# Strassen's seven products on two of eight k pairs of a gate/up projection in a fused decoder layer

## The chip, the cores and the metric

One core of one Trainium2 chip runs the whole layer as one program. The metric is the device time of an execution in microseconds, median of three. TensorE multiplies (PE in the profile), ScalarE (ACT) and VectorE (DVE) prepare its operands, SyncE (SP) issues the loads of the weights from HBM, and GpSimd (POOL) has little to do.

## The reference

A decoder layer over 256 tokens with a model width of 2048. What the change touches is the SwiGLU part with `D_FF = 5632`:

```
hn = rms_norm(h, ffn_norm[i])
h = h + (jax.nn.silu(hn @ w_gate[i]) * (hn @ w_up[i])) @ w_down[i]
```

Before it stand the combined projection, the two head groups and `w_o`, behind it a gated embedding (`w_ple_gate`, `w_ple_proj`). All inputs and weights are float32.

## The kernel before, in words

Each float32 operand is split into a rounded part (`hi`, type fp32r) and the remainder (`lo`), and each product is made as three matmuls: hi·hi, hi·lo, lo·hi (`k_tile`, lines 559 to 561). The stationary operand of a matmul is a 128x128 piece of the transposed activations `xT_hi` or `xT_lo` (one k tile of 128 rows, one half of the tokens), the moving one a 128x512 piece of weights.

The weights come in **units**: two k tiles by 512 columns, 512 KB, one DMA each. A unit goes through a ring of four buffers: SP loads `raw`, ACT rounds it into `w_hi` (line 915), DVE subtracts to `w_lo` (line 1226), PE multiplies. SP may load unit u when DVE is done with unit u-4 (`lo_ready`), ACT may round unit u when PE is done with unit u-4 (`unit_used`), PE waits for `lo_ready` of its unit. ACT and DVE work three units ahead of PE (`LEAD`). A unit is 12 matmuls.

A **gate/up block** makes 512 columns of gate and of up: eight units of `w_gate` into the two PSUM banks `pair[0]` (one for each half of the tokens), then eight units of `w_up` into `pair[1]`. There are eleven blocks: six (`FF_A`), then their down projection, five (`FF_B`), and theirs. The first block of either stage is written out ("peeled"), the five and four others are the body of a hardware loop. Behind the gate's last unit ACT makes the sigmoid and DVE the SiLU into `gate_s` (lines 1171 and 1525), which frees `pair[0]`. Behind the block DVE multiplies by up into `act_s` (line 1531), which frees `pair[1]`. In the next block PE transposes `act_s` into two spare banks behind its fourth unit (`turn_act`, line 829), and ACT and DVE split the result (`turned`, lines 1154 and 1509). All engines execute their instructions in the written order, and semaphores join them; nothing is reordered by a scheduler.

Of the kernel before, what the change touches and what calls it, by code (L numbers as in the profile page):

```python
# [24 lines left out]
ALU = mybir.AluOpType  # L25
# [70 lines left out]
def plan():  # L96
# [75 lines left out]
LAST_PIECES = ((0, 0, CB), (1, 0, CB // 2), (1, CB // 2, CB))  # L172


def build(nc, A):
    FIRST, AT, BANK_OF = plan()

    with ExitStack() as ctx:
# [63 lines left out]
        pp = sb("pp", [P, NT, D], at=res + 16 * KIB)  # L242
        sq = [sb(f"sq{t}", [P, CB]) for t in range(NT)]
# [4 lines left out]
        p_in = sb("p_in", [P, NT, PLE])  # L248
        pT_hi = sb("pT_hi", [P, PLE // P, TOK], F32R)
# [70 lines left out]
        ff_full, ff_free = [sem("ff_full0"), sem("ff_full1")], [sem("ff_free0"), sem("ff_free1")]  # L320
        pg_mul, out_ready, pg_full = sem("pg_mul"), sem("out_ready"), sem("pg_full")
# [64 lines left out]
        def _(sp):  # L386
            def load(u, j, w, k, col):

                if not isinstance(u, int) or u >= RING:
                    sp.wait_ge(lo_ready, u - (RING - 1))  # L390
                sp.dma_start(raw[j % RING][:], w[:, k:k + KU, bass.ds(col, CB)]).then_inc(raw_landed[j % RING], 16)
# [156 lines left out]
        def _(pe):  # L548
# [282 lines left out]

            def gate_up(i, u0, b0, n0, peeled):

                for j in range(2 * UPB):
                    use(i * (2 * UPB) + (u0 + j))
                    bl = j // UPB
                    if j % UPB == 0:

                        pe.wait_ge(pair_free[bl], i * 2 + b0)
                    for kk in range(KU):  # L840
                        k = KU * (j % UPB) + kk
                        if peeled and n0 == 0 and k in (0, 12):
                            for g in (range(6) if k == 0 else (6, 7)):
                                wait_read(pe, ("hA", g))
                        last = k_tile(j, kk, xT_hi[:, k, :], xT_lo[:, k, :], pair[bl], k == 0, k == KT - 1)
                        if kk == KU - 1:
                            last.then_inc(unit_used, 1)
                        if peeled:
                            for s in AT[u0 + j][kk]:
                                burst(s)  # L850
                    if j == 3 and not peeled:
                        pe.wait_ge(pair_free[1], i * 2 + b0)
                        turn_act()

            for n, n0, ug, ud, bgt, bd in ((FF_A, 0, U_GUA, U_DA, B_GUA, B_DA), (FF_B, FF_A, U_GUB, U_DB, B_GUB, B_DB)):
                gate_up(0, ug, bgt, n0, True)
                with pe.Fori(1, n) as i:
                    gate_up(i, ug, bgt, n0, False)
                def turn_last():
                    pe.wait_ge(pair_free[1], bd)  # L860
                    turn_act()
# [42 lines left out]
        def _(act):  # L904
# [13 lines left out]
            def post(step, b, half=None):  # L918
# [237 lines left out]

            def gate_up(i, u0, b0, n0, peeled):
                for j in range(2 * UPB):
                    split(i * (2 * UPB) + (u0 + j + LEAD), j + LEAD)
# [6 lines left out]
                    if j == UPB - 1:  # L1166
                        act.wait_ge(h_rstd, 2)
                        act.wait_ge(unit_used, i * (2 * UPB) + (u0 + UPB))
                        act.wait_ge(pair_free[1], i * 2 + b0)
                        for t in range(NT):  # L1170
                            f(gate_s[t][:], pair[0][t][:], ACT.Sigmoid, scale=h_rs[0][:, t:t + 1]).then_inc(gate_sig, 1)
# [48 lines left out]
        def _(dve):  # L1220
# [15 lines left out]
            def post(step, b, half=None):  # L1236
# [7 lines left out]
                if step in ("x", "hA", "hB"):  # L1244
                    col = {"x": G_ATTN, "hA": G_FFN, "hB": G_PLE}[step]
                    dve.wait_ge(x_hi, hi_base[step] + 2 * b + (1 if half == 0 else 2))
                    for kk in (0, 1) if half is None else (half,):
# [263 lines left out]

            def gate_up(i, u0, b0, n0, peeled):
                for j in range(2 * UPB):
                    split(i * (2 * UPB) + (u0 + j + LEAD), j + LEAD)
# [6 lines left out]
                    if j == UPB - 1:  # L1521
                        dve.wait_ge(h_rstd, 2)
                        for t in range(NT):
                            dve.wait_ge(gate_sig, i * 2 + (2 * n0 + t + 1))
                            v.scalar_tensor_tensor(out=gate_s[t][:], in0=pair[0][t][:], scalar=h_rs[0][:, t:t + 1],
                                                   in1=gate_s[t][:], op0=ALU.mult, op1=ALU.mult).then_inc(pair_free[0], 1)
                    if j == 2 * UPB - 1:
                        dve.wait_ge(unit_used, i * (2 * UPB) + (u0 + 2 * UPB))
                        dve.wait_ge(pair_free[0], i * 2 + (b0 + 2))
                        for t in range(NT):  # L1530
                            v.scalar_tensor_tensor(out=act_s[t][:], in0=pair[1][t][:], scalar=h_rs[0][:, t:t + 1],
# [66 lines left out]
```

## Time and profile before

| | |
|---|---|
| median of 3 runs | 1337.19 us (1337.16 to 1338.31) |
| profiled execution | 1338.08 us |
| its span | 1336.1 us |
| busy, share of the span | PE 100%, DVE 59%, ACT 47% |
| HBM read | 235.36 MB, 178 GB/s |

The profiled execution is 0.9 us over the median; its span leaves 2.0 us of it outside. "Busy" of PE overlaps, since a matmul's record is longer than the distance to the next one, so the pace of PE is read from start to start.

### The profile page before, as it was taken

The numbers are of one execution on the slowest core, as the hardware profiler recorded it, in microseconds if no ns is written. First come the engines' busy times: TensorE is split into PE (matmuls) and PEld (weight loads), VectorE is DVE, ScalarE is ACT, GpSimd is POOL, SyncE is SP. The second block draws the span as 40 slices with busy tenths as digits, with TensorE's granted clock in tenths as the row PEclk, the third lists the DMA queues.
The fourth block names the chain that finished last, engine by engine and source line by source line (L and its number), as shares of the span: only waits on it lengthen the run. The fifth ranks groups of instructions, "written<-read, shape, count | busy, mean of one in ns | idle before, by whom it ended". The sixth has DMA issues, their size and how long they took to land.

```text
span 1336.1 us, 18200 instructions
## 1 busy us (share of the span) xinstructions
PE 1330.2 (100%) x6774; PEld 1100.3 (82%) x6774; DVE 789.3 (59%) x987; ACT 626.8 (47%) x788; POOL 53.6 (4%) x71
## 2 busy tenths in 40 slices
PE   9999999999999999999999999999999999999998
PEld 8788888887888888888888888888888888888887
DVE  6578885788585555555555554444555555555554
ACT  6576444543555545444444443334444444444543
POOL 4002000220000000000000000000000000000000
PEclk9999999999999999999999999999999999999999
DMA  8555544554444555665666555566656665555564
GB/s 267 173 178 169 149 142 136 153 154 138 131 130 150 187 190 181 197 190 188 188 190 189 187 188 194 193 198 190 189 189 189 188 187 189 188 189 187 191 191 141
DMA packets 126201, 238.35 MB, mean 178 GB/s; under 512 B 9711, under 2 KB 10786, under 8 KB 126138
## 3 DMA queue, kind: packets, MB, share of 16 engines
q1 hardware_dynamic: 126106, 237.48, 56.8%
q8 instruction: 43, 0.70, 0.2%
q14 instruction: 20, 0.16, 0.0%
q10 hardware_dynamic: 32, 0.01, 0.0%
HBM read 235.36 MB, written 2.10 MB: 178 GB/s over the span
## 4 chain that ended last, share of the span: by engine, by line
PE 99%; DMA 0%; DVE 0%; ACT 0%; issue 0%
PE pair L559 30%; PE pair L561 30%; PE pair L560 30%; PE bg L679 2%; PE bg L744 2%; PE bg L615 1%; PE bg L829 1%; PE bg L725 0%; PE bg L592 0%; PE pair L898 0%; PE pair L897 0%; PE pair L899 0%; PE bg L643 0%; PE bg L650 0%; PE bg L659 0%; DMA row_a<-in_attn_norm_dram 0%
## 5 line engine op out<-in xcount | busy, mean ns | idle before, releaser
L1226 DVE TENSOR_TENSOR w_lo<-raw,w_hi 128x1024 fp32r<-128x1024 f32 x442 | 540.1, 1225 | 420.7 <-ACT w_hi L915 417.8
L915 ACT ACTIVATE w_hi<-raw 128x1024 fp32r<-128x1024 f32 x442 | 467.1, 1059 | 487.1 <-PE pair L561 483.5
L559 PE MATMUL pair<-w_hi,xT_hi 128*128 128x512 f32 x1264 | 503.1, 398 | 0.0
L561 PE MATMUL pair<-w_hi,xT_lo 128*128 128x512 f32 x1264 | 493.3, 390 | 0.0
L560 PE MATMUL pair<-w_lo,xT_hi 128*128 128x512 f32 x1264 | 492.7, 390 | 0.0
L561 PEld LDWEIGHTS pair<-w_hi,xT_lo 128*128 128x128 f32 x1264 | 237.4, 188 | 50.5
L559 PEld LDWEIGHTS pair<-w_hi,xT_hi 128*128 128x128 f32 x1264 | 237.7, 188 | 47.9
L560 PEld LDWEIGHTS pair<-w_lo,xT_hi 128*128 128x128 f32 x1264 | 237.9, 188 | 46.0
L559 PE MATMUL pair<-w_hi,actT_hi 128*128 128x512 f32 x352 | 137.7, 391 | 0.0
L561 PE MATMUL pair<-w_hi,actT_lo 128*128 128x512 f32 x352 | 137.1, 389 | 0.0
L560 PE MATMUL pair<-w_lo,actT_hi 128*128 128x512 f32 x352 | 137.0, 389 | 0.0
L561 PEld LDWEIGHTS pair<-w_hi,actT_lo 128*128 128x128 f32 x352 | 66.1, 188 | 13.9
L560 PEld LDWEIGHTS pair<-w_lo,actT_hi 128*128 128x128 f32 x352 | 66.1, 188 | 13.5
L559 PEld LDWEIGHTS pair<-w_hi,actT_hi 128*128 128x128 f32 x352 | 66.1, 188 | 13.4
L470 POOL TENSOR_SCALAR h_ms<-h_s 128x2 f32<-128x2 f32 x2 | 0.4, 192 | 845.7 <-DVE h_s L1493 845.7
L1296 DVE SCALAR_TENSOR_TENSOR mn<-bg,convw,mn 128x255 f32<-128x255 f32 (+2 forms) x72 | 29.6, 472 | 5.4 <-ACT mn L986 5.4
L1249 DVE SCALAR_TENSOR_TENSOR xT_lo<-bg,gains,xT_hi 128x256 fp32r<-128x256 f32 x47 | 20.6, 479 | 17.4 <-ACT xT_hi L946 17.3
L946 ACT ACTIVATE xT_hi<-bg,gains 128x256 fp32r<-128x256 f32 x47 | 19.8, 471 | 17.8 <-PE bg L615 15.7
L559 PE MATMUL pair<-w_hi,og_hi 128*128 128x512 f32 x64 | 25.9, 405 | 0.0
L559 PE MATMUL pair<-w_hi,om_hi 128*128 128x512 f32 x64 | 25.2, 394 | 0.0
L1509 DVE TENSOR_TENSOR actT_lo<-bg,actT_hi 128x512 f32 (+1 forms) x22 | 14.2, 686 | 18.4 <-ACT actT_hi L1154 18.4
L561 PE MATMUL pair<-w_hi,og_lo 128*128 128x512 f32 x64 | 25.0, 391 | 0.0
(234 smaller groups left out, 876.8 us busy)
## 6 DMA issues: line engine op xcount, KB each, us to landing
raw<-in_w_in_dram SPq DMA_DIRECT2D x112, 512.0 KB, 3.7
raw<-in_w_gate_dram SPq DMA_DIRECT2D x88, 512.0 KB, 4.4
raw<-in_w_up_dram SPq DMA_DIRECT2D x88, 512.0 KB, 3.9
raw<-in_w_down_dram SPq DMA_DIRECT2D x88, 512.0 KB, 4.7
raw<-in_w_o_dram SPq DMA_DIRECT2D x32, 512.0 KB, 4.2
raw<-in_w_ple_gate_dram SPq DMA_DIRECT2D x32, 512.0 KB, 4.1
raw<-in_w_ple_proj_dram SPq DMA_DIRECT2D x4, 512.0 KB, 4.7
h<-in_x_dram SPq DMA_DIRECT2D x3, 512.0 KB, 8.7
```

Source lines behind the costliest of these rows:

```text
L559: mm(banks[t][:], hi[:, ts], wh, start=first, stop=False)
L560: mm(banks[t][:], hi[:, ts], wl, start=False, stop=False)
L561: m = mm(banks[t][:], lo[:, ts], wh, start=False, stop=last)
L615: m = tp(o[:, kk * TOK + t * P:kk * TOK + t * P + P], h[:, t, k * P:(k + 1) * P], ident[:])
L679: m = mm(out[r][rs, j, :], lhs, rhs, start=True, stop=True)
L744: last = mm(o, l, r, start=True, stop=True)
L915: f(w_hi[j % RING][:], raw[j % RING][:], ACT.Copy).then_inc(hi_ready, 1)
L946: f(xT_hi[:, k, :], (x1_bank if half else bk)[:, kk * TOK:(kk + 1) * TOK], ACT.Copy, scale=gains[:, col + k:col + k + 1]).then_inc(x_hi, 1)
L1226: v.tensor_tensor(w_lo[j % RING][:], raw[j % RING][:], w_hi[j % RING][:].bitcast(F32), ALU.subtract).then_inc(lo_ready, 1)
L1249: m = v.scalar_tensor_tensor(out=xT_lo[:, k, :], in0=(x1_bank if half else bk)[:, kk * TOK:(kk + 1) * TOK], scalar=gains[:, col + k:col + ...
L1296: v.scalar_tensor_tensor(out=o, in0=src, scalar=convw[:, t0 * CONV + tap:t0 * CONV + tap + 1], in1=o, op0=ALU.mult, op1=ALU.add).then_inc( ...
L1509: v.tensor_tensor(actT_lo[:, ks, :], bg[q][:].rearrange("p (k n) -> p k n", k=2), actT_hi[:, ks, :].bitcast(F32), ALU.subtract).then_inc(f ...
```

## The change

In each block the pairs of k tiles 3 and 4 of eight (`MIXED`) are multiplied by Strassen's scheme. The 2x2 matrix on the left is token half by k tile, that on the right is k tile by gate or up, and seven 128x128x512 products take the place of eight. The left forms (`F_hi`, `F_lo`) are made once, where `hn` is transposed (steps `hA`). The right forms are made anew in each block from the raw gate unit and the raw up unit of the pair: t3, t1, t2 and t4, four dependent subtractions on DVE, which are then rounded by ACT and split by DVE like weights (`t_hi`, `t_lo`). The scheme leaves sums in the banks, so the other up units add up differences of token halves (`d_hi`, `d_lo`), and DVE adds three spare banks back in at the end of gate and of up. The order of the units (`SEQ`) becomes six gate units, the pair 3 (gate, up), three up units, the pair 4, three up units. The raw gate buffer of a pair holds t2 and t4 until they are split, so its next load waits for `t24_lo_ready`.

```diff
+MIXED = (3, 4)
+PLAIN = [g for g in range(UPB) if g not in MIXED]
+SEQ = ([("gate", g) for g in PLAIN[:4]] + [("gate", g) for g in PLAIN[4:]] + [("gate", MIXED[0]), ("up", MIXED[0])]
+       + [("up", g) for g in PLAIN[:3]] + [("gate", MIXED[1]), ("up", MIXED[1])] + [("up", g) for g in PLAIN[3:]])
...
-            at[U_WO + (n + 1) * UPB + 2][g].append(("hA", 2 * n + g))
+            at[U_WO + (n + 1) * UPB + (2 if n < 3 else 1)][g].append(("hA", 2 * n + g))
...
 # SP
+                    for j, (side, g) in enumerate(SEQ):
+                        w = w_gate if side == "gate" else w_up
+                        if j >= RING and SEQ[j - RING] in [("gate", m) for m in MIXED]:
+                            sp.wait_ge(t24_lo_ready, i * 2 + (2 * at + MIXED.index(SEQ[j - RING][1]) + 1))
+                            fetch(j, w, KU * g, i * CB + at * CB)
+                        else:
+                            load(i * (2 * UPB) + (u0 + j), j, w, KU * g, i * CB + at * CB)
...
 # PE
+            def product(o, hi, lo, wh, wl, first, last):
+                mm(o, hi, wh, start=first, stop=False)
+                mm(o, hi, wl, start=False, stop=False)
+                return mm(o, lo, wh, start=False, stop=last)
+            def mixed_units(u, j, q, n):
...
+                use(u)
+                product(bg[0][:], xT_hi[:, k0, a0], xT_lo[:, k0, a0], gh[:, 0, :], gl[:, 0, :], first, last)
+                product(pair[0][0][:], xT_hi[:, k1, a0], xT_lo[:, k1, a0], gh[:, 1, :], gl[:, 1, :], False,
+                        last).then_inc(unit_used, 1)
+                use(u + 1)
+                product(pair[1][1][:], F_hi[:, q, 0, :], F_lo[:, q, 0, :], uh[:, 0, :], ul[:, 0, :], first, False)
+                product(pair[1][0][:], F_hi[:, q, 2, :], F_lo[:, q, 2, :], uh[:, 1, :], ul[:, 1, :], first,
+                        False).then_inc(unit_used, 1)
+                pe.wait_ge(t3_lo_ready, n)
+                product(bg[2][:], F_hi[:, q, 3, :], F_lo[:, q, 3, :], t_hi[:, 2, :], t_lo[:, 2, :], first, last)
+                pe.wait_ge(t24_lo_ready, n)
+                product(bg[1][:], F_hi[:, q, 1, :], F_lo[:, q, 1, :], t_hi[:, 0, :], t_lo[:, 0, :], first, last)
+                product(pair[0][1][:], xT_hi[:, k1, a1], xT_lo[:, k1, a1], t_hi[:, 1, :], t_lo[:, 1, :], False,
+                        last).then_inc(t_used, 1)
...
+                    if j == 0:
+                        pe.wait_ge(pair_free[0], i * 2 + b0)
...
-                    if j == 3 and not peeled:
+                    if j == 2 and not peeled:
                         pe.wait_ge(pair_free[1], i * 2 + b0)
+                        pe.wait_ge(gate_sum, i * 2 + 2 * n0)
                         turn_act()
...
 # ACT
+            def split_mixed(u, j, n, n0_first):
+                jg = (j - 1) % RING
+                act.wait_ge(t3_ready, n)
+                if not n0_first:
+                    act.wait_ge(t_used, n - 1)
+                f(t_hi[:, 2, :], t3_raw[:], ACT.Copy).then_inc(t3_hi_ready, 1)
+                act.wait_ge(t1_ready, n)
+                act.wait_ge(unit_used, u - (RING - 1))
+                f(w_hi[j % RING][:], raw[j % RING][:], ACT.Copy).then_inc(hi_ready, 1)
+                act.wait_ge(t4_ready, n)
+                f(t_hi[:, 0:2, :], raw[jg][:], ACT.Copy).then_inc(t24_hi_ready, 1)
...
+                    if j == 13:
+                        act.wait_ge(t_used, i * 2 + (2 * n0 + 2))
+                        f(act_s[1][:], bg[0][:], ACT.Copy).then_inc(p1_copied, 1)
...
 # DVE
+            def split_mixed(u, j, n):
+                jg, ju = (j - 1) % RING, j % RING
+                dve.wait_ge(lo_ready, u)
+                dve.wait_ge(raw_landed[ju], (u - ju) * (16 // RING) + 16)
+                v.tensor_tensor(t3_raw[:], raw[ju][:, 1, :], raw[ju][:, 0, :], ALU.subtract).then_inc(t3_ready, 1)
+                dve.wait_ge(t3_ready, n)
+                v.tensor_tensor(raw[ju][:, 0, :], raw[ju][:, 0, :], raw[jg][:, 0, :], ALU.subtract).then_inc(t1_ready, 1)
+                dve.wait_ge(t1_ready, n)
+                v.tensor_tensor(raw[jg][:, 0, :], raw[ju][:, 1, :], raw[ju][:, 0, :], ALU.subtract).then_inc(t2_ready, 1)
+                dve.wait_ge(t2_ready, n)
+                v.tensor_tensor(raw[jg][:, 1, :], raw[jg][:, 1, :], raw[jg][:, 0, :], ALU.subtract).then_inc(t4_ready, 1)
+                split(u, j)
+                dve.wait_ge(t3_hi_ready, n)
+                v.tensor_tensor(t_lo[:, 2, :], t3_raw[:], t_hi[:, 2, :].bitcast(F32), ALU.subtract).then_inc(t3_lo_ready, 1)
+                dve.wait_ge(t24_hi_ready, n)
+                v.tensor_tensor(t_lo[:, 0:2, :], raw[jg][:], t_hi[:, 0:2, :].bitcast(F32),
+                                ALU.subtract).then_inc(t24_lo_ready, 1)
```

On DVE, in the loop's body, this is what stands behind `turned` in the changed kernel (`raw_54` holds the pair's up unit, `raw_53` its gate unit, `t_raw` is t3):

```order
L1667 TENSOR_TENSOR actT_lo<-bg,actT_hi 128x512
L1674 ISA [waits lo_ready]
L1675 TENSOR_TENSOR t_raw<-raw_54 128x512 [waits raw_landed3]
L1676 ISA
L1677 TENSOR_TENSOR raw_54<-raw_54,raw_53 128x512 [waits t3_ready]
L1679 TENSOR_TENSOR raw_53<-raw_54 128x512 [waits t1_ready]
L1681 TENSOR_TENSOR raw_53<-raw_53 128x512 [waits t2_ready]
L1350 REGISTER_ALU
L1351 TENSOR_TENSOR w_lo_62<-raw_54,w_hi_58 128x1024 [waits hi_ready]
L1684 TENSOR_TENSOR t_lo<-t_raw,t_hi 128x512 [waits t3_hi_ready]
L1686 TENSOR_TENSOR t_lo<-raw_53,t_hi 128x1024 [waits t24_hi_ready]
```

Before, one row `w_lo` stood in the place of these nine of DVE from L1674 to L1686.

On DVE, the end of the block in the loop's body. Before, between the last units' splits and the branch:

```order
L1226 TENSOR_TENSOR w_lo_60<-raw_52,w_hi_56 128x1024 [waits hi_ready]
L1225 REGISTER_ALU
L1226 TENSOR_TENSOR w_lo_61<-raw_53,w_hi_57 128x1024 [waits hi_ready]
L1529 REGISTER_ALU [waits unit_used]
L1531 SCALAR_TENSOR_TENSOR act_s_90<-pair,h_rs_196,gate_s_88 128x512 [waits pair_free0]
L1531 SCALAR_TENSOR_TENSOR act_s_91<-pair,h_rs_196,gate_s_89 128x512
```

And in the changed kernel (`v_s`, `u_s` are the running sums; `w_lo_59` is the first unit of the next block):

```order
L1351 TENSOR_TENSOR w_lo_59<-raw_51,w_hi_55 128x1024 [waits hi_ready]
L1705 REGISTER_ALU
L1706 TENSOR_TENSOR v_s<-bg,act_s_91 128x512 [waits p1_copied]
L1707 TENSOR_TENSOR gate_s_88<-pair,act_s_91 128x512
L1709 TENSOR_TENSOR u_s<-bg,v_s 128x512 [waits v_ready]
L1711 TENSOR_TENSOR gate_s_89<-pair,u_s 128x512 [waits v_ready]
L1350 REGISTER_ALU
L1351 TENSOR_TENSOR w_lo_60<-raw_52,w_hi_56 128x1024 [waits hi_ready]
L1716 SCALAR_TENSOR_TENSOR gate_s_88<-gate_s_88,h_rs_209,act_s_90 128x512 [waits gate_sig,h_rstd]
L1716 SCALAR_TENSOR_TENSOR gate_s_89<-gate_s_89,h_rs_209,act_s_91 128x512 [waits gate_sig]
```

The SiLU, which frees `pair[0]`, moved from behind the split of the block's 11th unit (three ahead of the eight gate units) to behind that of the next block's second unit, and four sums stand ahead of it.

On SP, in the loop's body of the changed kernel, the loads of units 9 to 12 (counted from 0; before, all sixteen loads of a block waited for `lo_ready` alone):

```order
L425 DMA raw_52<-in_w_up_dram 128x2x512 [waits lo_ready]
L464 ISA
L425 DMA raw_53<-in_w_up_dram 128x2x512 [waits t24_lo_ready]
L420 REGISTER_ALU
L425 ISA [waits lo_ready]
L425 DMA raw_54<-in_w_gate_dram 128x2x512
L420 REGISTER_ALU
L425 DMA raw_51<-in_w_up_dram 128x2x512 [waits lo_ready]
```

The load of unit 10 waits for the last split of the pair (behind it in DVE's order: `t_lo<-raw_53`), and units 11 and 12, which follow in SP's order, can't go ahead of it. The same stands once more at unit 15, ahead of the next block's first loads.

## Rows read from the trace of the kernel before

**Rows 1.** The page: busy time of PE, its clock in 40 slices, the chain.

```profile
PE 1330.2 (100%) x6774; PEld 1100.3 (82%) x6774; DVE 789.3 (59%) x987; ACT 626.8 (47%) x788; POOL 53.6 (4%) x71
PEclk9999999999999999999999999999999999999999
PE 99%; DMA 0%; DVE 0%; ACT 0%; issue 0%
```

**Rows 2.** Timeline of PE, one gate unit and `turn_act` behind it (start, us).

```profile
642.22 0.39 PE L559 MATMUL pair<-w_hi,xT_hi 128*128 128x512 f32 x1
642.45 0.39 PE L560 MATMUL pair<-w_lo,xT_hi 128*128 128x512 f32 x1
...
644.94 1.03 PE L829 MATMUL bg<-ident,act_s 128*128 128x128 f32 x8
645.73 0.48 PE L559 MATMUL pair<-w_hi,xT_hi 128*128 128x512 f32 x1
```

**Rows 3.** Timeline of ACT over one block (start, us).

```profile
612.64 1.27 ACT L1171 ACTIVATE gate_s<-pair,h_rs 128x512 f32<-128x512 f32 x2 [1.80 <-PE pair L561]
...
642.42 1.06 ACT L915 ACTIVATE w_hi<-raw 128x1024 fp32r<-128x1024 f32 x1 [1.66 <-PE pair L561]
645.69 1.09 ACT L1154 ACTIVATE actT_hi<-bg 128x512 f32 x2 [2.21 <-PE bg L829]
...
657.05 1.27 ACT L1171 ACTIVATE gate_s<-pair,h_rs 128x512 f32<-128x512 f32 x2 [1.80 <-PE pair L561]
```

**Rows 4.** Timeline of DVE in the same block.

```profile
643.51 1.23 DVE L1226 TENSOR_TENSOR w_lo<-raw,w_hi 128x1024 fp32r<-128x1024 f32 x1 [1.50 <-ACT w_hi L915]
646.46 1.29 DVE L1509 TENSOR_TENSOR actT_lo<-bg,actT_hi 128x512 f32 x2 [1.73 <-ACT actT_hi L1154]
...
657.78 1.41 DVE L1525 SCALAR_TENSOR_TENSOR gate_s<-pair,h_rs,gate_s 128x512 f32<-128x512 f32 x2 [1.27 <-ACT gate_s L1171]
```

**Rows 5.** Timeline of DVE in the last stage: dependent and independent operations of 128x512.

```profile
1267.08 0.69 DVE L1573 TENSOR_TENSOR gate_s<-gate_s,pp 128x512 f32<-128x512 f32 x1 [1.07 <-ACT gate_s L1216]
1267.81 0.69 DVE L1575 TENSOR_TENSOR h<-h,gate_s 128x512 f32<-128x512 f32 x1
1268.42 0.68 DVE L1573 TENSOR_TENSOR gate_s<-gate_s,pp 128x512 f32<-128x512 f32 x1
...
1269.74 2.35 DVE L1226 TENSOR_TENSOR w_lo<-raw,w_hi 128x1024 fp32r<-128x1024 f32 x2
```

**Rows 6.** Who waited for whom, 560 to 760 us (total, times, longest).

```profile
ACT w_hi L915 <- PE pair L561: 96.6, 64, 1.7
DVE w_lo L1226 <- ACT w_hi L915: 77.4, 59, 1.6
```

**Rows 7.** DMA issues from 638 to 646 us: median us to landing.

```profile
raw<-in_w_up_dram SPq DMA_DIRECT2D x3, 512.0 KB, 4.3
```

**Rows 8.** Two loads 1.57 us apart: their issues, then their landing.

```profile
616.14 0.37 SPq L391 DMA_DIRECT2D raw<-in_w_up_dram  x1
617.71 0.38 SPq L391 DMA_DIRECT2D raw<-in_w_gate_dram  x1
...
raw<-in_w_up_dram SPq DMA_DIRECT2D x1, 512.0 KB, 3.4
raw<-in_w_gate_dram SPq DMA_DIRECT2D x1, 512.0 KB, 4.2
```

**Rows 9.** Two loads 1.14 us apart in w_o: their issues, then their landing.

```profile
438.06 0.37 SPq L391 DMA_DIRECT2D raw<-in_w_o_dram  x1
439.20 0.37 SPq L391 DMA_DIRECT2D raw<-in_w_o_dram  x1
...
raw<-in_w_o_dram SPq DMA_DIRECT2D x1, 512.0 KB, 3.9
raw<-in_w_o_dram SPq DMA_DIRECT2D x1, 512.0 KB, 5.6
```

**Rows 10.** Rate of all DMA engines in 40 slices of 612 to 621 us.

```profile
GB/s 328 119 18 0 0 137 118 218 300 355 391 400 301 100 9 0 0 0 0 0 0 0 0 109 173 209 255 382 419 382 291 164 91 82 155 246 355 382 410 328
```

**Rows 11.** Timelines of ACT and DVE around the first gate/up block's start.

```profile
508.18 0.84 ACT L946 ACTIVATE xT_hi<-bg,gains 128x256 fp32r<-128x256 f32 x2 [0.68 <-PE bg L615]
523.67 1.28 ACT L1171 ACT_TABLE_LOAD   x1 [1.63 <-PE pair L561]
...
509.05 0.88 DVE L1249 SCALAR_TENSOR_TENSOR xT_lo<-bg,gains,xT_hi 128x256 fp32r<-128x256 f32 x2 [0.29 <-ACT xT_hi L946]
```

More of the change, by code:

```diff
@@ L390, in load, with fetch @@
                     sp.wait_ge(lo_ready, u - (RING - 1))
+                fetch(j, w, k, col)
+            def fetch(j, w, k, col):
                 sp.dma_start(raw[j % RING][:], w[:, k:k + KU, bass.ds(col, CB)]).then_inc(raw_landed[j % RING], 16)
@@ new lines, in gate_up @@
+            def gate_up(i, u0, b0, n0, peeled):
+                for j, (side, g) in enumerate(SEQ):
+                    u = i * (2 * UPB) + (u0 + j)
+                    if g in MIXED:
+                        if side == "up":
+                            continue
+                        q = MIXED.index(g)
+                        if q == 0:
+                            pe.wait_ge(pair_free[1], i * 2 + b0)
+                            if not peeled:
+                                for n in range(2):
+                                    pe.wait_ge(ff_free[n], i + n0)
+                        mixed_units(u, j, q, i * 2 + (2 * n0 + q + 1))
+                        continue
+                    use(u)
+                    if j == 0:
+                        pe.wait_ge(pair_free[0], i * 2 + b0)
+                    if peeled and n0 == 0 and g in (PLAIN[0], 6) and side == "gate":
+                        for n in (range(6) if g == PLAIN[0] else (6, 7)):
+                            wait_read(pe, ("hA", n))
+                    for kk in range(KU):
+                        k = KU * g + kk
+                        wh, wl = w_hi[j % RING][:, kk, :], w_lo[j % RING][:, kk, :]
+                        if side == "gate":
+                            last = k_tile(j, kk, xT_hi[:, k, :], xT_lo[:, k, :], pair[0], k == 0, False)
+                        else:
+                            d = KU * PLAIN.index(g) + kk
+                            product(pair[1][1][:], xT_hi[:, k, P:TOK], xT_lo[:, k, P:TOK], wh, wl, False, k == KT - 1)
+                            last = product(pair[1][0][:], d_hi[:, d, :], d_lo[:, d, :], wh, wl, False, k == KT - 1)
@@ L947, in post @@
                           scale=gains[:, col + k:col + k + 1]).then_inc(x_hi, 1)
+                    if step == "hA":
+                        q = PLAIN.index(b)
+                        act.wait_ge(d_ready, q + 1)
+                        for kk in range(2):
+                            k = 2 * b + kk
+                            f(d_hi[:, 2 * q + kk, :], d_raw[:, kk, :], ACT.Copy,
+                              scale=gains[:, col + k:col + k + 1]).then_inc(d_rounded, 1)
                 elif step == "p":
@@ L1155, in turned @@
                       ACT.Copy).then_inc(act_hi_ready, 1)
+            def split_mixed(u, j, n, n0_first):
[9 more added lines that the diff above has]
+                f(t_hi[:, 0:2, :], raw[jg][:], ACT.Copy).then_inc(t24_hi_ready, 1)
             def gate_up(i, u0, b0, n0, peeled):
                 for j in range(2 * UPB):
-                    split(i * (2 * UPB) + (u0 + j + LEAD), j + LEAD)
+                    u = i * (2 * UPB) + (u0 + j + LEAD)
+                    side, g = SEQ[j + LEAD] if j + LEAD < 2 * UPB else ("gate", 0)
+                    if side == "up" and g in MIXED:
+                        q = MIXED.index(g)
+                        split_mixed(u, j + LEAD, i * 2 + (2 * n0 + q + 1), peeled and n0 == 0 and q == 0)
+                    else:
+                        split(u, j + LEAD)
                     if peeled:
```

127 lines of the change are left out of this document (104 added, 23 removed).

## Prediction

> **What bounds the kernel now.** I read the page first. PE is busy all the span and the chain that ended last is 99% PE [rows 1], with the clock at its upper level (2.4 GHz) in every slice. A matmul's own record (0.39 us) is no measure, since records overlap, so the pace comes from PE's timeline: a unit of 12 matmuls starts at 642.22 and the next work at 644.94, 2.72 us, or 0.2266 us for each [rows 2]. The eight transposes of `turn_act` add 645.73 - 644.94 = 0.8 us, and 0.1 us more on the matmul behind them, 0.9 us in all. The block's period can be read on ACT, from sigmoid to sigmoid: 657.05 - 612.64 = 44.41 us [rows 3], and 192 x 0.2266 + 0.9 = 44.41. So PE loses nothing in a block today. The waits say the same from the other side: ACT waits for PE 64 times in 200 us and DVE for ACT [rows 6]; nobody waits for DVE or a load. That slack is what the change spends.
>
> **What it removes.** Each pair needs 7 x 3 = 21 matmuls for 24. Six fewer a block, 11 blocks, 66 matmuls: 66 x 0.2266 = **-15.0 us**. All are of one shape, 128x512 on a 128x128 stationary, as before, so there is no cheaper or dearer kind among them. The plain up units keep 12 matmuls, `turn_act` only moves. Loads are as many and as large. A block without stalls is 44.41 - 1.36 = 43.05 us.
>
> **What it adds on DVE.** Durations of 128x512: 0.61 us from start to start when independent, 0.73 when each needs the one before [rows 5]; a split of 128x1024 is 1.23 us, 1.13 from start to start (two in 2.35) [rows 5]. A pair adds four dependent subtractions (2.9 us) and splits of 512 and 1024 columns (0.6 + 1.2), 4.7 us. Two pairs 9.4; the sums at the gate's end 2.5, at the up's end 1.9. With 16 splits, `turned` 1.3 and the two multiplications 1.4 each [rows 4] that is 36 us of DVE in 43. Busy time alone would fit. The question is the order, so I follow one loop block in time, PE's first matmul of it at 0.
>
> - 8.16: PE ends unit 2 (3 x 2.72). 0.2 us later (642.22 to 642.42) ACT rounds unit 6, 1.06 us [rows 3]; DVE splits it until 10.6. `turned` follows on DVE, two halves in 1.29 [rows 4]: 11.8.
> - 11.8 to 14.7: the four subtractions. Then split of unit 7 (1.13), of t3 (0.61), of t2 and t4 (1.23): **17.6**. PE comes to unit 6 at 17.2 and to t3 and t2/t4 at 19.9 and 20.6, so the pair itself doesn't stall.
> - 17.6: only now can SP load unit 10, and unit 11 right behind it (an issue holds the queue 0.37 us [rows 8]). Before, unit 10's buffer was free when unit 6 was split, at 10.6. Let x be the time from the first issue to the landing of the second load. Unit 10 itself is in time: landing 3.4 us later [rows 8], split 2.3 after that at 23.4, wanted at 27.4.
> - 17.6 + x: unit 11 (gate of pair 4) is there. ACT 1.06, DVE split 1.13, four subtractions 2.9, splits 1.13 + 0.61 + 1.23: 8.0 in all with the hand-overs. **25.6 + x**: SP loads unit 15 and, right behind it, the next block's unit 0. y is again the second's landing.
> - 25.6 + x + y: ACT 1.1, DVE split of that unit 1.13, the four gate sums 2.55, the next split 1.13, the SiLU 1.4: 7.35 in all. Only then is `pair[0]` free: **33.0 + x + y**.
>
> The next block's first matmul needs it at 43.05. So the stall of a loop block is x + y - 10.1 where that is over nothing. The pair doubles x and y: this is the one sensitive number.
>
> **x and y.** No row shows two loads 0.37 us apart after a pause. From the nearest: loads in the usual cadence take 4.3 us [rows 7], so 0.4 + 4.3 = 4.7 if the second behaves like any other. Two loads 1.57 apart: the second is there 1.57 + 4.2 = 5.8 after the first's issue. Two 1.14 apart in the `w_o` stage: 1.14 + 5.6 = 6.7 [rows 8, 9]. The engines move at most about 400 GB/s [rows 10], 1.3 us for 512 KB, so with the first there at 3.4 the second can't be before 4.7 either. Ends 4.7 and 6.7. The middle row is of the same stage and loop and differs only in a later second issue, which can only make its landing later; so I take less, **5.4**. Stall: 0.7 us in each of the 9 loop blocks, +6.3 us. In the two peeled blocks there is no `turned` ahead of the subtractions, 1.3 us less, so no stall. The down projection behind a stage waits for `pair[0]` too and counts as the next block.
>
> The Trainium skill (DMA: Bandwidth & Descriptors, Anatomy of one DMA) fits a DMA, measured on another issue path, as a fixed 2.0 us and bytes over 436 GB/s. If of two queued loads only the second part adds up, that makes 3.2 us for the first load here and 4.4 for the second, an estimate by that page. By that, x + y = 8.8, no stall, and the whole 15 us would come in. The trace's 3.4 us for a load after a pause agrees nearly, its 5.8 and 6.7 do not.
>
> **Edges.** The `hA` steps carry more: behind ACT's 0.84 us and DVE's 0.88 [rows 11] come a copy, a difference, two roundings and two splits of 128x128 each, about as much again. They lie beside the `w_o` matmuls, all but the last two. Those go one unit earlier and are wanted at the fifth unit instead of the seventh; by my sum DVE is done with them about 10.5 us into the block, and the fifth unit starts at 11. The load of the sigmoid's table, 1.28 us [rows 11], moves to the block's end, where the sigmoid has over 1 us of slack. 0.6 us for both, between 0 and 2.
>
> **Sum.** -15.0 + 6.3 + 0.6 = -8.1 us on a span of 1336.1. The profiled execution (1338.08) is 0.9 us over the median of the runs, and I carry the difference over to the median of 1337.19: **1329 us**.
>
> **The rivals.**
> - *The second load lands cleanly behind the first* (x and y at most 5.0). No stall: 1337.2 - 15.0 = 1322 us. For it the peak rate of [rows 10]; against it both pairs of [rows 8, 9], in which the second took 4.2 and 5.6 us from its own issue though 1.14 us apart leave room. 0.25.
> - *Mine*, x and y from 5.0 to 5.7: the loop blocks stall 0 to 1.3 us, 1323 to 1334.5, 1329 the likeliest. 0.4.
> - *Balance*, 5.7 to 5.95: the stalls eat the matmuls (9 x 1.6 in the loops, 2 x 0.3 in the peeled blocks at 5.85), within 2.7 us of 1337. 0.15.
> - *Slower*: the second load behaves as in [rows 8] or worse. At x = y = 6.0 the stall is 1.9 in loop blocks and 0.6 in peeled ones, 18.3 us: 1341. At 6.7, the row of `w_o`, 3.3 and 2.0: 34 us, 1356. It decides from x + y = 11.7 on, where 9 stalls of 1.6 and two of 0.3 and the edges make 15. What speaks for it is that these are measured; what speaks against it is that each had a later second issue, and that the `w_o` stage runs unrolled code. 0.2.
> - A stall elsewhere, at PE's wait for t2 and t4: they are ready 3 us ahead at pair 3; at pair 4 they are ready at 25.6 + x = 31.0 and PE wants them at 30.1 + 2.72 + 0.68 = 33.5. It bites only beyond x = 7.9. Part of the slower case. That the matmuls aren't saved I exclude by the order: 186 stand where 192 stood.
>
> **How the numbers follow.** A median of this kernel can tell about 0.2%, 2.7 us, from no change. Faster by more: the first two cases nearly whole, 0.64. Within: 0.15. Slower: 0.21. The range goes from the clean case with a little room, 1321.5, up to x about 6.0, 1342; above lies about half of the slower case and 0.04 lie below. My own case alone is 1323 to 1334.5.
>
> **What would show it.** In the changed kernel's profile PE should be idle at the first matmul of a block, released by DVE's SiLU, for about 0.7 us each time in the loops and nowhere else in a block; blocks should follow each other at 43.7 us. The waits should have ACT's rounding wait for a load (units 10, 11, 15 and 0) some 2 to 3 us each. The landing of the second load of a pair says x at once. If no PE wait shows, x was under 5. If PE waits inside a pair, my order of DVE is wrong. If the clock falls in a slice, the stalls cost more than their own length. DVE should stand at about 80% in a block.

## The result, and the profile after

| | before | changed |
|---|---|---|
| median (6 runs each) | 1337.35 us | 1346.63 us (1343.89 to 1349.59) |
| ratio | | 1.0068, 95% interval 1.0058 to 1.0078 |
| profiled execution | 1338.08 us | 1346.31 us |
| its span | 1336.1 us | 1344.4 us |

The changed kernel is 0.7% slower, not 0.6% faster. The page of the changed kernel, its row of busy times and its chain, to be held against [rows 1]:

```profile
PE 1322.8 (98%) x6708; PEld 1089.4 (81%) x6708; DVE 931.5 (69%) x1222; ACT 675.6 (50%) x865; POOL 54.7 (4%) x71
...
PE 70%; DVE 13%; DMA 8%; issue 4%; ACT 3%; SPq 1%; DVEq 0%; ACTq 0%
```

The 66 matmuls are gone (6774 to 6708), but PE no longer makes up the whole chain: DVE has 13% of it and DMA 8%. The waits of the whole execution (total, times, longest) say where PE stands:

```profile
ACT w_hi L999 <- DMA raw<-in_w_up_dram: 71.5, 22, 3.8
...
ACT w_hi L999 <- DMA raw<-in_w_gate_dram: 16.1, 23, 2.3
PE pair L597 <- DVE gate_s L1716: 15.6, 11, 2.3
```

PE waits 11 times, once in each block, and only for the SiLU (`gate_s`, L1716) that frees `pair[0]`. ACT waits 22 times for an up unit, which is unit 10 or 15 of each of 11 blocks. ACT's timeline over the end of one loop block shows both halves of the chain:

```profile
657.26 1.06 ACT L999 ACTIVATE w_hi<-raw 128x1024 fp32r<-128x1024 f32 x1 [2.97 <-DMA raw<-in_w_up_dram]
658.56 1.06 ACT L999 ACTIVATE w_hi<-raw 128x1024 fp32r<-128x1024 f32 x1 [0.24 <-DMA raw<-in_w_gate_dram]
...
670.36 1.06 ACT L999 ACTIVATE w_hi<-raw 128x1024 fp32r<-128x1024 f32 x1 [3.15 <-DMA raw<-in_w_up_dram]
673.71 1.06 ACT L999 ACTIVATE w_hi<-raw 128x1024 fp32r<-128x1024 f32 x1 [2.29 <-DMA raw<-in_w_gate_dram]
```

These four are units 10, 11, 15 and the next block's unit 0. The second of the first two keeps ACT 0.24 us, the second of the other two 2.29 us. DVE's timeline behind them:

```profile
661.01 0.69 DVE L1675 TENSOR_TENSOR t_raw<-raw 128x512 f32<-128x512 f32 x1
...
665.54 1.22 DVE L1686 TENSOR_TENSOR t_lo<-raw,t_hi 128x1024 fp32r<-128x1024 f32 x1
...
674.81 1.23 DVE L1351 TENSOR_TENSOR w_lo<-raw,w_hi 128x1024 fp32r<-128x1024 f32 x1 [2.13 <-ACT w_hi L999]
675.95 0.68 DVE L1706 TENSOR_TENSOR v_s<-bg,act_s 128x512 f32<-128x512 f32 x1
...
678.47 1.22 DVE L1351 TENSOR_TENSOR w_lo<-raw,w_hi 128x1024 fp32r<-128x1024 f32 x1
679.61 1.41 DVE L1716 SCALAR_TENSOR_TENSOR gate_s<-gate_s,h_rs,act_s 128x512 f32<-128x512 f32 x2
```

It is the order of the prediction: the last split of the pair at 665.54, the loads (666.79 and 667.79, below), then the sums at 675.95, a split, and the SiLU at 679.61. PE's last matmul of the block had started at 678.64. The issues of the two loads, and their landing from issue:

```profile
666.79 0.37 SPq L425 DMA_DIRECT2D raw<-in_w_up_dram  x1
667.79 5.42 SPq L425 DMA_DIRECT2D raw<-in_w_gate_dram  x4
...
raw<-in_w_up_dram SPq DMA_DIRECT2D x1, 512.0 KB, 3.6
raw<-in_w_gate_dram SPq DMA_DIRECT2D x1, 512.0 KB, 5.8
```

The second is issued 1.00 us after the first (its row merges it with three later loads) and takes 5.8 us, so y, the time from the first issue to the second landing, is 6.8 in this block.

The second thing that is new is the clock. PE's timeline at the start of the second gate/up block:

```profile
542.96 0.39 PE L874 MATMUL pair<-w_hi,d_lo 128*128 128x512 f32 x1
545.63 0.50 PE L597 MATMUL pair<-w_hi,xT_hi 128*128 128x512 f32 x1 [2.28 <-DVE gate_s L1716]
...
546.71 0.63 PE L598 MATMUL pair<-w_lo,xT_hi 128*128 128x512 f32 x1
547.13 0.63 PE L599 MATMUL pair<-w_hi,xT_lo 128*128 128x512 f32 x1
```

PE stood for 2.28 us. One microsecond after it came back, the distance from matmul to matmul is 0.42 us in place of 0.23. The table of stretches, with the granted clock in the third column from the end:

```profile
546.00:551.00 5.00, 5.00 (x17) 3.96 (x16) 4.96 (x7) 1.11 (x2) 0.00 (x0) 0.66 0.64 199
771.00:776.00 5.00, 5.00 (x17) 3.91 (x16) 4.95 (x7) 0.88 (x1) 0.00 (x0) 0.66 0.54 191
1126.00:1131.00 5.00, 4.46 (x13) 3.51 (x14) 5.00 (x8) 0.69 (x1) 0.00 (x0) 0.66 0.65 206
```

A granted clock of 0.66 over 5 us is 3.4 us at the lower level (1.2 GHz) and the rest at the upper. Each stretch holds 8 matmuls, 0.43 us apart where 0.23 would do: 1.6 us lost. There are three, each behind a stall of 2.2 us or more; two more of 2.2 and 2.3 us (at 678.64 and 1078.43) brought none. Before, the clock stood at its upper level up to the last 3.8 us. The sign doesn't hang on the clock: of the six executions of the changed kernel one had a mean granted clock of 0.999, which is the kernel before's own, and took 1345.42 us.

**The account.** From PE's starts, what the distance at the head of the next block exceeds the usual 0.23 us by, block by block: 2.44, 1.55, 0.43, 2.20, 0.94, 2.20 in the first stage and 0.96, 1.58, 0.39, 2.30, 2.37 in the second, 17.4 us in all. The next three matmuls behind each of these heads start 0.13 us late together, 1.4 us in all. -15.0 (matmuls) + 17.4 (stalls) + 1.4 (behind them) + 3 x 1.6 (clock) = +8.6 us; the spans differ by 8.3. Nothing is hidden elsewhere: held against `early` below, whose PE runs the same 6708 matmuls in the same order without a stall, distance by distance, the changed kernel's 23.6 us more are 17.4 at the heads, 1.4 behind them, 4.8 at the lower clock and 0.0 in the sum of all other distances.

### The profile page after: what moved, and what is told of

It is laid out like the page before. It is cut to its first block, busy times and chain, and to the rows that moved or that the text cites. A ratio compares the mean times of both kernels' runs of the same rounds, so it can differ in the third digit from the quotient of the medians.

```text
span 1344.4 us, 18516 instructions
## 1 busy us (share of the span) xinstructions
PE 1322.8 (98%) x6708; PEld 1089.4 (81%) x6708; DVE 931.5 (69%) x1222; ACT 675.6 (50%) x865; POOL 54.7 (4%) x71
## 4 chain that ended last, share of the span: by engine, by line
PE 70%; DVE 13%; DMA 8%; issue 4%; ACT 3%; SPq 1%; DVEq 0%; ACTq 0%
PE pair L597 21%; PE pair L599 20%; PE pair L598 20%; DMA raw<-in_w_gate_dram 7%; DVE w_lo L1351 4%; DVE t_lo L1686 2%; ACT w_hi L999 2%; PE bg L717 2%; PE bg L782 2%; DVE gate_s L1716 1%; DVE raw L1677 1%; DVE raw L1679 1%; DVE t_raw L1675 1%; DMA raw<-in_w_down_dram 1%; PE bg L653 1%
## 5 line engine op out<-in xcount | busy, mean ns | idle before, releaser
L999 ACT ACTIVATE w_hi<-raw 128x1024 fp32r<-128x1024 f32 x420 | 442.4, 1059 | 417.2 <-PE pair L599 317.5
L597 PE MATMUL pair<-w_hi,xT_hi 128*128 128x512 f32 x824 | 333.1, 404 | 11.5 <-DVE gate_s L1716 11.3
L599 PE MATMUL pair<-w_hi,xT_lo 128*128 128x512 f32 x824 | 322.6, 392 | 0.0
L598 PE MATMUL pair<-w_lo,xT_hi 128*128 128x512 f32 x824 | 322.2, 391 | 0.0
L597 PEld LDWEIGHTS pair<-w_hi,xT_hi 128*128 128x128 f32 x824 | 155.2, 188 | 46.5 <-DVE gate_s L1716 15.1
L599 PEld LDWEIGHTS pair<-w_hi,xT_lo 128*128 128x128 f32 x824 | 155.1, 188 | 33.5
L598 PEld LDWEIGHTS pair<-w_lo,xT_hi 128*128 128x128 f32 x824 | 155.3, 188 | 28.7
L872 PE MATMUL pair<-w_hi,xT_hi 128*128 128x512 f32 x154 | 59.9, 389 | 0.0
L873 PE MATMUL pair<-w_lo,xT_hi 128*128 128x512 f32 x154 | 59.9, 389 | 0.0
L874 PE MATMUL pair<-w_hi,xT_lo 128*128 128x512 f32 x154 | 59.9, 389 | 0.0
L872 PE MATMUL pair<-w_hi,d_hi 128*128 128x512 f32 x132 | 51.3, 389 | 0.0
L873 PE MATMUL pair<-w_lo,d_hi 128*128 128x512 f32 x132 | 51.3, 389 | 0.0
L874 PE MATMUL pair<-w_hi,d_lo 128*128 128x512 f32 x132 | 51.3, 389 | 0.0
```

What stands on the lines that cost most here:

```text
L597: mm(banks[t][:], hi[:, ts], wh, start=first, stop=False)
L598: mm(banks[t][:], hi[:, ts], wl, start=False, stop=False)
L599: m = mm(banks[t][:], lo[:, ts], wh, start=False, stop=last)
L872: mm(o, hi, wh, start=first, stop=False)
L873: mm(o, hi, wl, start=False, stop=False)
L874: return mm(o, lo, wh, start=False, stop=last)
```

## The experiments

The theory: PE has lost nothing but waits for `pair[0]`; they come from the chain split of t2/t4, two loads, four sums, SiLU, and the clock falls because of them. Its rivals: DVE's extra work slows PE in other ways; the matmuls are worth less than 0.2266 us; the second load's lateness is a matter of what is loaded. The kernel before, timed beside all of them, took 1337.7 us (1337.15 to 1338.47).

| kernel | median us (5 rounds) | ratio to before, 95% | PE's stalls, us | half-clock stretches |
|---|---|---|---|---|
| changed (6 runs) | 1346.63 | 1.0068 [1.0058, 1.0078] | 17.4 | 3 |
| early | 1322.64 | 0.9887 [0.9872, 0.9902] | 0 | 0 |
| sums | 1328.45 | 0.9928 [0.9914, 0.9941] | 4.9 | 1 |
| swapboth | 1352.20 | 1.0103 [1.0087, 1.0120] | 21.7 | 3, one twice as long |
| extra | 1343.08 | 1.0039 [1.0026, 1.0053] | 5.5 | 0 |
| unroll | 1332.41 | 0.9957 [0.9943, 0.9971] | 8.0 | 0 |
| early_sums | 1322.75 | 0.9886 [0.9871, 0.9902] | 0 | 0 |
| early_extra | 1338.12 | 1.0002 [0.9993, 1.0011] | 0 | 0 |
| late | 1365.60 | 1.0223 [1.0202, 1.0244] | 29.6 | 7 |

Stalls (the excess at the eleven heads) and stretches (of 3.4 us each; the last microseconds, which every kernel has at a lower clock, are left out) are those of the profiled execution.

### early: the loads don't wait for the splits

t2 and t4 get a buffer of their own, so the gate's `raw` buffer is free when t4 is made, not when it is split.

```
+        t24_raw = sb("t24_raw", [P, 4, CB], at=mix + 56 * KIB)
...
-                            sp.wait_ge(t24_lo_ready, i * 2 + (2 * at + MIXED.index(SEQ[j - RING][1]) + 1))
+                            sp.wait_ge(t4_ready, i * 2 + (2 * at + MIXED.index(SEQ[j - RING][1]) + 1))
...
-                v.tensor_tensor(raw[jg][:, 0, :], raw[ju][:, 1, :], raw[ju][:, 0, :], ALU.subtract).then_inc(t2_ready, 1)
+                v.tensor_tensor(t24_raw[:, 0, :], raw[ju][:, 1, :], raw[ju][:, 0, :], ALU.subtract).then_inc(t2_ready, 1)
-                v.tensor_tensor(raw[jg][:, 1, :], raw[jg][:, 1, :], raw[jg][:, 0, :], ALU.subtract).then_inc(t4_ready, 1)
+                v.tensor_tensor(t24_raw[:, 3, :], raw[jg][:, 1, :], t24_raw[:, 0, :], ALU.subtract).then_inc(t4_ready, 1)
...
```

> The edit: t2 and t4 are written to a tile of their own instead of over the raw gate unit, and SP may load units 10 and 15 when t4 is made (t4_ready) instead of when it is split (t24_lo_ready), 2.9 us sooner in the order of DVE. Same work on every engine. Theory A (one chain through DVE and two loads, from PE's unit 2 to the SiLU that frees the gate's banks, is longer than PE's block): the loads leave 2.9 us sooner each and no longer two at once, the chain falls under PE's 43.05 us, no PE wait at a block's start, no half clock, 1323 us (1337.4 - 15.0 + 0.6). Theory B (PE loses in the scheme itself: its products or its waits for t2/t4): no change, 1346. Theory C (DVE has too much work in a block, wherever it stands): no change, 1346.

Measured: 1322.64 us, 24.0 less than the changed kernel. The page:

```profile
PE 1314.8 (100%) x6708; PEld 1087.3 (82%) x6708; DVE 936.2 (71%) x1222; ACT 677.4 (51%) x865; POOL 54.8 (4%) x71
...
PE 99%; DMA 0%; DVE 0%; ACT 0%; issue 0%
```

All of the chain is PE again, with the same work on DVE. The span is 1320.8 us; 1336.1 - 15.0 = 1321.1. The seven products alone are worth what the prediction said, and the earlier release of one buffer is enough to take the whole loss away: unit 10 is issued 14.7 us into a loop block and not 17.7, and the SiLU is over 1.6 us before PE wants `pair[0]`.

### sums: the SiLU a split earlier

The copy on ACT, and the four sums on DVE in the same way, move ahead of the operation on a unit that stood before them; loads and waits stay.

```
+                    if j == 13:
+                        act.wait_ge(t_used, i * 2 + (2 * n0 + 2))
+                        f(act_s[1][:], bg[0][:], ACT.Copy).then_inc(p1_copied, 1)
...
-                    if j == 13:
-                        act.wait_ge(t_used, i * 2 + (2 * n0 + 2))
-                        f(act_s[1][:], bg[0][:], ACT.Copy).then_inc(p1_copied, 1)
```

> The edit: ACT's copy and DVE's four gate sums stand ahead of the split of the next block's unit 0 instead of behind it, so DVE makes them while it waits for that unit's load. Same work. Theory A: 2.5 us of DVE leave the chain behind the load, but some of it moves into DVE's way; about 1.2 us less stall a block, from 1.6 to 0.6 us or less, no half clock: 1329 to 1333 us. Theories B (PE loses in the scheme) and C (too much DVE work): 1346.

Measured: 1328.45 us, 18.2 less. Stalls of 4.9 us are left (2.45 at the first block's end, eight between 0.1 and 0.5) and one half-clock stretch: 1336.1 - 15.0 + 4.9 + 1.6 = 1327.6 on a span of 1329.0. The profiled execution is the longest of the five (1330.96 us); the mean granted clock of the other four is 1.000, so they have no such stretch. So the chain can be cut at its far end just as well; it is its length that counts.

### swapboth: the loads of each pair in the other order

Units 11 and 10, and the next block's unit 0 and 15, change places in SP's order, so that the gate unit comes first. SP's loop is written out for it.

```
+                order = (*range(1, 10), 11, 10, 12, 13, 14)
...
+                    load(i * (2 * UPB) + (u0 + 2 * UPB), 0, w_gate, KU * SEQ[0][1], i * CB + (at + 1) * CB)
+                    unit(i, 15)
```

> The edit: SP issues the load of unit 11 ahead of that of unit 10, and that of the next block's unit 0 ahead of that of unit 15 (SP's program is written out instead of looped for that). The buffers' waits are the same, only SP's order changes. Theory A: the second of two loads is there when the first is, x falls from 5.3 to about 4.0 to 4.5 and y from 6.0 to about 5, but DVE still splits in the old order: 0.5 to 1.2 us less stall a block, 1331 to 1339 us. Theories B and C: 1346.

Measured: 1352.2 us, 5.6 over the changed kernel and 19.8 over the one with the written-out loop alone (`unroll`, below). The expectation missed. SP's issues, and ACT's timeline:

```profile
655.64 0.37 SPq L425 DMA_DIRECT2D raw<-in_w_gate_dram  x1
...
669.93 0.37 SPq L425 DMA_DIRECT2D raw<-in_w_gate_dram  x1
671.67 0.37 SPq L425 DMA_DIRECT2D raw<-in_w_up_dram  x1
```

```profile
662.31 2.01 ACT L1012 ACTIVATE w_hi<-raw 128x1024 fp32r<-128x1024 f32 x2 [4.01 <-DMA raw<-in_w_up_dram]
...
676.42 2.01 ACT L1012 ACTIVATE w_hi<-raw 128x1024 fp32r<-128x1024 f32 x2 [4.66 <-DMA raw<-in_w_up_dram]
```

ACT and DVE still take unit 10 before 11 and 15 before 0. Unit 15 is issued at 671.67 and rounded from 676.42: as the second load it needs 4.7 us, where as the first it needed 3.6 (rounded at 670.36, issued at 666.79). And the other unit's rounding (x2, back to back) now lies behind that wait instead of in the shadow of the second landing. Against `unroll`, stalls are 13.7 us longer and the lost clock about 6.4; the spans differ by 20.1. What I had overlooked is that an earlier gate unit is of no use to consumers that go in order.

### extra: the matmuls given back

Three matmuls a pair more, into a spare bank that is never read; PE has 6774 matmuls again.

```
+                product(bg[3][:], F_hi[:, q, 1, :], F_lo[:, q, 1, :], t_hi[:, 0, :], t_lo[:, 0, :], True, True)
```

> The edit: behind the product with t2 PE multiplies it once more into a spare bank, three matmuls for each pair that nobody reads, so that PE has as many matmuls as before the change (66 more). Theory A: the chain through DVE sets the block, and PE does them in the time in which it stood: a stall of 1.6 us shrinks to 0.3, blocks with less stall than 1.36 us get longer; +2.7 us from those, up to -5 from half clock that doesn't come: 1342 to 1349 us. Theory B (PE-bound with a cost of its own in the scheme): +15 us, 1361.

Measured: 1343.08 us. With 15.0 us more of matmuls the kernel is 3.5 us *faster* than the changed one: the stalls fall from 17.4 to 5.5 us and the half-clock stretches from three to none, together -16.7 against +15.0 (the spans differ by -2.0). In the changed kernel, then, the matmuls saved bring nothing: the time is set by the chain around them, and PE merely waits longer.

### unroll: only SP's loop written out

```
-                with sp.Fori(0, n) as i:
+                for i in range(n):
                     for j, (side, g) in enumerate(SEQ):
```

> Only SyncE's loop over the gate/up blocks is written out instead of being a hardware loop; every load, wait and order stays. In the changed kernel the two loads that are issued together inside a block lie 0.63 us apart and the second is there 5.3 us after the first's issue; the two at the block's end, with the loop's branch between them, lie 0.9 to 1.1 us apart and the second is there after 6.0 us on average. Theory A (y is longer because the second issue comes later): the gap falls to about 0.6 us, y to about 5.3, the stalls shrink by 0.7 us in nine loop blocks, and with fewer of them over 2 us the half-clock stretches go too: 1334 to 1340 us. Rival B (y is longer because of what is loaded, the first unit of a new column block, or by the state of the queue, not by the gap): y stays at 6.0 and the time within 2 us of the changed kernel's 1346.6.

Measured: 1332.41 us, 14.2 less, below the forecast of 1334 to 1340. SP's issues of unit 15 and of the next block's first units, and the landings, at the same place in the program as above:

```profile
663.88 0.37 SPq L425 DMA_DIRECT2D raw<-in_w_up_dram  x1
664.30 7.43 SPq L425 DMA_DIRECT2D raw<-in_w_gate_dram  x5
```

```profile
raw<-in_w_up_dram SPq DMA_DIRECT2D x1, 512.0 KB, 3.7
raw<-in_w_gate_dram SPq DMA_DIRECT2D x1, 512.0 KB, 4.6
```

The second follows after 0.42 us and y is 5.0. In the nine blocks whose next one is in the same loop, y is 4.96 to 5.15. In the two whose next load belongs to the down projection's loop, 0.72 and 0.74 us later, it is 6.23 and 5.52, and the first of these has the longest stall, 1.75 us. Whether the distance or the matrix makes the difference there, no run separates. That speaks against rival B: the same new column block lands 0.8 us sooner on average (5.07 for 5.86) once it is issued 0.6 us sooner. So does `early`: there the second load of both pairs is issued 1.27 to 1.48 us behind the first, and lands at 5.98 us on average for unit 11 and at 6.02 for the next block's unit 0. No stall reaches 2 us and the clock never falls: 1336.1 - 15.0 + 8.0 + 1.4 (behind the heads) = 1330.5, which is the span.

### early_sums: both cures

The edits of `early` and `sums` together.

> Both cures of the late SiLU at once: t2 and t4 have a buffer of their own, so that the loads don't wait for their splits, and the gate's sums stand one split earlier. Theory A (the early release alone has already taken all of PE's waits away, what is left is PE's own 6708 matmuls): the same as the early release alone, 1322 to 1323.5 us. Rival B (PE still loses small amounts that the profile's rows don't show as waits): 1 to 3 us less than the early release alone.

Measured: 1322.75 us, as `early` alone. Nothing of the change's cost is left for a shorter chain to save.

### early_extra: DVE's work by itself

`early` with the matmuls of `extra`.

> The early release with three more matmuls in each pair (the third of a block's wait-free products repeated into a spare bank that is never read), so PE has the 6774 matmuls of the kernel before while DVE keeps all additions of the scheme. Theory A (the matmuls removed are worth 66 x 0.2266 us, and DVE's additions cost nothing when nobody waits for them): 1322.6 + 15.0 = 1337.6, equal to the kernel before within 1.5 us. Rival B (DVE's 21 percent more work slows PE by sharing memory or otherwise costs): over 1340 us.

Measured: 1338.12 us, 15.5 over `early` and level with the kernel before (1.0002, interval 0.9993 to 1.0011), though DVE is busy 19% longer than before, with 1222 instructions for 987. So 66 matmuls are worth 15.5 us (15.0 by the prediction), and DVE's additions cost nothing while nobody waits for them. Rival B falls.

### late: the chain made longer

Two additions of 128x512 into a buffer that is never read stand among the gate's sums.

```
+                        v.tensor_tensor(pad[:], bg[1][:], p1[:], ALU.add)
                         v.tensor_tensor(v_s[:], bg[1][:], p1[:], ALU.add).then_inc(v_ready, 1)
...
+                        v.tensor_tensor(pad[:], bg[2][:], v_s[:], ALU.add)
                         v.tensor_tensor(gate_s[1][:], pair[0][1][:], u_s[:], ALU.add).then_inc(gate_sum, 1)
```

> The changed kernel with two more additions of 128x512 on DVE among the gate's sums, whose result nobody reads: the SiLU comes 1.2 us later in each of the 11 blocks. Theory A (each stall grows by what is late, and stalls of 2 us and more bring stretches at half clock, 1.7 us lost for each stretch of 3.4 us): 11 x 1.2 = 13.2 us of longer stalls, and at most blocks now over 2 us, so some 3 to 8 more half-clock stretches, 5 to 14 us: 1365 to 1374 us, and a mean granted clock of 0.985 to 0.99. Rival B (the clock is not tied to the stalls): 1359 to 1361 us, clock 0.995.

Measured: 1365.6 us, 19.0 over the changed kernel. The wait for the SiLU in the whole execution, and two of the stretches behind it:

```profile
PE pair L598 <- DVE gate_s L1719: 27.8, 11, 3.7
```

```profile
640.00:645.00 5.00, 3.95 (x11) 3.15 (x12) 5.00 (x8) 1.19 (x2) 0.00 (x0) 0.66 0.62 189
688.00:693.00 5.00, 5.00 (x15) 3.94 (x16) 5.00 (x7) 0.49 (x2) 0.00 (x0) 0.66 0.62 203
```

The stalls grew by 29.6 - 17.4 = 12.2 us (11 x 1.2 = 13.2 expected), the stretches from three to seven, 4 x 1.6 = 6.4 us; 18.6 together, the spans differ by 18.7. Without the clock, 6 us of it would be unexplained, so rival B falls here too.

## Why the prediction was wrong

**Right.** The matmuls' worth: 15.0 by the sum, 15.5 measured (`early_extra` less `early`). The place and the releaser of the stall: the head of a block, DVE's SiLU, nowhere within a pair. ACT's waits for units 10 and 15, 3.0 and 3.15 us (but 0.24 for unit 11, the second landing being close behind the first). x = 5.4: measured 5.16 to 5.52, mean 5.3. DVE at 80% of a block (142.4 of 178 us from 590 to 768). The table's load costs nothing in the first block: it lies at 541.87 to 543.15 on ACT, and the SiLU can't start before the split at 543.03 is over at 544.16.

**Wrong: "x and y", the choice of 5.4 for both.** I took the two pairs of loads for alike, since the order shows SP's instructions side by side in both. They aren't: the second pair has the end of SP's hardware loop between its issues, and with it they lie 0.88 to 1.09 us apart and not 0.63. y was 6.05 on average in the nine loop blocks (4.95 to 6.84). That is worth 9 x 0.65 = 5.9 us less 9 x 0.1 on x. The row I started from was also no typical one. I read 5.8 us for two loads 1.57 us apart from the one pair of [rows 8] and argued that a sooner second issue can only land sooner. That pair is the fastest of nine at its place in the kernel before: they land 5.74 to 6.83 us after the first issue, 6.14 on average. One of them, two blocks on:

```profile
705.00 0.37 SPq L391 DMA_DIRECT2D raw<-in_w_up_dram  x1
706.57 0.38 SPq L391 DMA_DIRECT2D raw<-in_w_gate_dram  x1
...
raw<-in_w_up_dram SPq DMA_DIRECT2D x1, 512.0 KB, 3.5
raw<-in_w_gate_dram SPq DMA_DIRECT2D x1, 512.0 KB, 4.8
```

That is 1.57 + 4.8 = 6.4 us, and a pair 0.99 us apart, at 506.31 us, lands at 6.12. [Rows 9], which I had set aside as code of another stage, would have misled the other way: pairs of `w_o` units 1.14 us apart land at 6.78 on average, pairs of up units at the same distance at 5.84 (table at the end).

Writing out SP's loop gave back 14 us (`unroll`, at 1332.4 within 4 us of the forecast of 1329), so the loop's time between issues alone turns the sign: 9.4 us of stalls and 4.8 of clock. It shortened the distance inside a block too (0.63 to 0.41 us, x from 5.30 to 5.22 on average), which is the smaller part. By my own formula, though, the right y would have given -3.2 us, nearly a tie; the rest to the account's +8.6 is in the three points below (10.3 us) and in the 1.4 us behind the heads. The nine loop blocks lasted 44.95 us on average, from head to head, not 43.7: longer than before (44.41).

**Mis-sized: 33.0 + x + y.** With the measured x and y the formula gives 1.25 us a loop block; the stalls were 1.55. The hand-overs of the chain were 0.3 us longer than the sum of its rows, +2.7 us: the first pair's last split ends 17.7 us into a block (17.6 forecast), the second's at 31.1 to 31.4 (30.9 with the measured x), the SiLU at 33.35 + x + y. (In the block that begins at the lower clock all three come 1.6 us later.)

**Wrong: "in the two peeled blocks ... so no stall".** I took the 1.3 us of `turned` off DVE's chain, but left the deadline at 43.05 although PE has no `turn_act` there either and comes 0.9 us sooner. The second peeled block stalled 0.96 us. The first stalled 2.44: its pair 3 is delayed by the `hA` steps. DVE's timeline there:

```profile
509.99 0.62 DVE L1406 SCALAR_TENSOR_TENSOR d_lo<-d_raw,gains,d_hi 128x128 fp32r<-128x128 f32 x2
510.94 2.36 DVE L1351 TENSOR_TENSOR w_lo<-raw,w_hi 128x1024 fp32r<-128x1024 f32 x2 [0.33 <-ACT w_hi L999]
513.34 0.69 DVE L1675 TENSOR_TENSOR t_raw<-raw 128x512 f32<-128x512 f32 x1
```

The last `hA` step was done at 510.6, as forecast ("about 10.5 us into the block", which began at 500.1), but the splits of units 5 and 6 stood behind it, and the subtractions began at 13.3 us into the block; in the other peeled block, at 10.8. Both blocks together: 3.4 us, where I had 0.6 for this edge and the table.

**Left out: the clock.** I had named it as something to look for, without a price: 4.8 us of the changed kernel's time, and 11.2 (7 x 1.6) of the 42 us by which the span of `late` exceeds 1321.1, PE's work alone. A stall of 2.2 us came to cost 3.8.

The rival *Slower* is the one that came about, though not by its own bound: it decides at x + y = 11.7, and the trace had 11.35. The hand-overs, the peeled blocks and the clock (2.7 + 2.8 + 4.8 us) carried it across. What I had held against it, that its rows "each had a later second issue", was the thing to check: the order gives the sequence of the issues and not their distance.

## What to carry to other kernels

When a change holds a buffer longer, follow the release through the next loads to the instruction that PE waits for, and give the temporaries a buffer of their own before counting what the saved matmuls bring: here that alone made -1.1% out of +0.7%. Two instructions that stand side by side in a queue's order aren't side by side in time if a hardware loop's end lies between them; look for such an end wherever a chain of waits passes a queue. Take more than one row for the term on which the sum hangs: the nine pairs at one place of the kernel before differed by 1.1 us, and I had read the fastest. And price a stall of PE's at more than its length once it comes near 2 us: 14 of the 20 stalls over 2 us here cost about 1.6 us of clock on top, one of them more.

## What the runs showed of the hardware

- **The second of two queued loads.** Two loads of 512 KB from one queue after a pause, over eight kernels (all but `swapboth` and the one before); the first four rows are units 10 and 11, and 15 and the next unit 0; the landing of the second from the issue of the first, by the distance of the issues:

| distance, us | pairs | mean | from, to | mean from its own issue |
|---|---|---|---|---|
| 0.41 to 0.42 | 20 | 5.16 | 4.96, 5.33 | 4.74 |
| 0.63 | 44 | 5.34 | 5.07, 5.89 | 4.71 |
| 0.88 to 1.09 | 44 | 5.96 | 4.95, 7.24 | 5.00 |
| 1.27 to 1.34 | 51 | 5.96 | 5.69, 7.02 | 4.69 |
| 1.13 to 1.14, two up units (7 and 8) | 73 | 5.84 | 5.02, 6.39 | 4.70 |
| 1.13 to 1.14, two units of `w_o` | 32 | 6.78 | 6.03, 7.26 | 5.64 |

  At 0.72 and 0.74 us there are only two, 6.23 and 5.52. For units of gate and up the mean hardly changes from 0.9 us on, and is lower at 0.63 and 0.41. The units of `w_o` land 0.9 us later at the same distance; why, no run tells. The first load of a pair takes 3.5 to 4.5. At 0.88 to 1.09 us the scatter is the widest: there the parts of one or a few of the 16 engines come 1 to 2 us behind the others (in the block with y = 6.8, 14 parts by 4.4 us after the issue and two at 5.7 and 5.8). Why, no run here tells. The Trainium skill (DMA: Bandwidth & Descriptors, Anatomy of one DMA) would by its fit, which is of another issue path, put the second at 4.4 us, an estimate; the trace has 5.2 at the smallest distance, and the measurement decides.
- **A hardware loop's end in SP's queue** put 0.5 to 0.7 us between two issues (0.88 to 1.09 against 0.41 written out), and a load inside the loop 0.2 us (0.63 against 0.41).
- **The clock.** Stalls over 2 us brought a stretch of 3.4 us (once 6.8) at the lower level (1.2 GHz) in three of five cases in the changed kernel, in seven of nine in `late`, in three of five in `swapboth` and in the one of `sums`; none followed a stall below 2 us in any of these, nor in `unroll` (11) and `extra` (7). It began between 0.7 us before PE came back and 1.4 us after. The Trainium skill (TensorE: Matmul & The Clock Gate, Part 1) puts the array at half its clock when PE has been idle; the granted clock of 0.66 over 5 us agrees. What makes one stall of 2.2 us cost a stretch and the next not stays open.
